# State space decays: one 64-row product a head, one limit by broadcast, four biased exponentials, the gate ahead of them and the scans one step later

## The reference

```
a_cum = cumsum(a, within chunks of 128 tokens)          # a = dt * (-exp(a_log)), 32 heads
seg = a_cum[..., :, None] - a_cum[..., None, :]
decay_in = exp(where(causal, seg, -inf))
cb = einsum('bctgn,bcsgn->bgcts', cc, bc)
y_diag = einsum('bgcts,bgrcts,bcsgrp->bctgrp', cb, decay_in, xc)
decay_to_end = exp(a_cum[..., -1:] - a_cum)
chunk_states = einsum('bctgn,bgrct,bctgrp->bcgrpn', bc, decay_to_end, xc)
# carry the states over the 4 chunks, then
y_off = einsum('bctgn,bcgrpn,bgrct->bctgrp', cc, entering, exp(a_cum))
```

## Time and profile before

| | |
|---|---|
| time, median of 3 runs | 1708.93 us (1708.85 to 1710.78) |
| the profiled execution | 1710.39 us, of which the span of the profile is 1708.6 us |
| TensorE busy | 1669.1 us, 98% of the span |
| VectorE busy | 973.3 us, 57% |
| ScalarE busy | 811.2 us, 47% |
| GpSimd busy | 688.7 us, 40% |
| granted TensorE clock, mean | 0.995 |

### The profile page before, as it was taken

The page is one execution under the profiler, slowest core; times in us unless marked ns, Lnnn a source line. Parts: engine busy times, 40 slices in busy tenths (PEclk is TensorE's granted clock), DMA queues, the critical chain, the costliest instruction groups (busy, mean ns, idle before and its releaser), DMA issues.

```text
span 1708.6 us, 23429 instructions
## 1 busy us (share of the span) xinstructions
PE 1669.1 (98%) x8992; PEld 1349.9 (79%) x8992; DVE 973.3 (57%) x1858; ACT 811.2 (47%) x1370; POOL 688.7 (40%) x905
## 2 busy tenths in 40 slices
PE   8999899999999999998999999999999999999998
PEld 8887567977988888887877777877788777787876
DVE  6489773533665757636656666167453554445445
ACT  5563753532644545424464444145455453534434
POOL 4555323422323342552455556455442333324440
PEclk9999999999999999999999999999999999999999
DMA  8423101221313231411221222211211312112201
GB/s 301 146 102 104 45 2 50 75 74 50 124 49 124 74 135 63 148 62 50 99 75 50 75 75 75 99 62 54 83 64 52 101 51 68 60 52 88 68 27 54
DMA packets 24807, 137.03 MB, mean 80 GB/s; under 512 B 2511, under 2 KB 5839, under 8 KB 11000
## 3 DMA queue, kind: packets, MB, share of 16 engines
q1 hardware_dynamic: 24696, 135.53, 23.0%
HBM read 133.40 MB, written 2.12 MB: 79 GB/s over the span
## 4 chain that ended last, share of the span: by engine, by line
PE 89%; DVE 5%; ACT 3%; issue 1%; DMA 0%; SPq 0%; DVEq 0%; ACTq 0%
PE ps L1660 85%; PE ps L1664 3%; DVE XL L2781 1%; ACT XH L2217 0%; DVE tmp L2708 0%; DVE LNS L2741 0%; PE ps L1668 0%; ACT whi L2217 0%; DVE XL L2785 0%; ACT L2217 0%; DVE ESG L2705 0%; DMA MEM<-memT 0%; DVE LG L2708 0%; DVE mb L2711 0%; ACT tmp L2217 0%
## 5 line engine op out<-in xcount | busy, mean ns | idle before, releaser
L3342 POOL TENSOR_TENSOR wlo<-raw,whi 128x256 fp32r<-128x256 f32 (+1 forms) x820 | 612.9, 784 | 841.2 <-ACT whi L2217 841.2
L2217 ACT ACTIVATE whi<-raw 128x2048 fp32r<-128x2048 f32 (+4 forms) x144 | 248.8, 1731 | 157.7 <-PE ps L1660 122.8
L1660 PE MATMUL ps<-XH,whi 128*128 128x512 f32 (+1 forms) x1176 | 298.5, 374 | 4.4 <-ACT XH L2217 4.2
L1660 PE MATMUL ps<-XL,whi 128*128 128x512 f32 (+1 forms) x1176 | 281.3, 361 | 0.1
L1660 PE MATMUL ps<-XH,wlo 128*128 128x512 f32 (+1 forms) x1176 | 280.6, 361 | 0.0
L1660 PEld LDWEIGHTS ps<-XH,whi 128*128 128x128 f32 x1176 | 200.9, 189 | 43.8 <-ACT XH L2217 6.8
L1660 PEld LDWEIGHTS ps<-XL,whi 128*128 128x128 f32 x1176 | 204.9, 189 | 35.0 <-DVE XL L2785 0.3
L1660 PEld LDWEIGHTS ps<-XH,wlo 128*128 128x128 f32 x1176 | 204.7, 189 | 34.1
L2812 DVE TENSOR_TENSOR R<-ps,R 128x512 f32<-128x512 f32 (+1 forms) x80 | 50.9, 636 | 134.3 <-PE ps L1660 133.7
L1660 PE MATMUL ps<-BH,whi 128*128 128x512 f32 (+1 forms) x320 | 89.4, 397 | 0.0
L1660 PE MATMUL ps<-BL,whi 128*128 128x512 f32 (+1 forms) x320 | 84.1, 380 | 0.8 <-DVE BL L3269 0.8
(11 more groups left out here) (388 smaller groups left out, 2992.5 us busy)
## 6 DMA issues: line engine op xcount, KB each, us to landing
raw<-wall SPq DMA_DIRECT2D x107, 1024.0 KB, 4.8
raw<-wall SPq DMA_DIRECT2D x11, 512.0 KB, 3.5
raw<-wall SPq DMA_DIRECT2D x8, 576.0 KB, 3.6
raw<-wall SPq DMA_DIRECT2D x4, 768.0 KB, 4.2
BFL<-scr SPq DMA_DIRECT2D x2, 1024.0 KB, 8.2
outN<-Y SPq DMA_DIRECT2D x8, 256.0 KB, 2.1
MEM<-memT SPq DMA_DIRECT2D x2, 512.0 KB, 5.0
XTA<-x SPq DMA_DIRECT2D x2, 512.0 KB, 9.4
```

What stands on the lines that cost most here:

```text
L1660: return nc.tensor.matmul(o_, l, r_, start=start, stop=stop, skip_group_check=True)
L2217: return nc.scalar.activation(o_, i_, func, bias=bias, scale=scale)
L3342: t = tt(wlo[u % NSPL][:, c], raw_of(u)[:, c], f32(whi[u % NSPL][:, c]), ALU.subtract)
```

## The change

sx: ACH and ACL become one tile `ACS` of 64 rows, and the identity `IDR` gets 64 rows and the sign -1, so that one product gives minus the spread a_cum. VectorE does one operation a head instead of four: the maximum of that and `NAC` (minus a_cum, broadcast along the chunk). ScalarE's exponentials take the scale -1; that of `ESG` is cut in four, each with its own column of `NAC` as bias. The bank of an sx step is still given back by the first exponential. Order of the list: `gate` is appended ahead of the four sx steps, and `turn` gets one more empty entry in third place, so that each scan piece and g3 and g4 come one main step later. In group 1 the gate and the sx steps of group 0 both stand behind step 4; before, the sx steps stood there and the gate behind step 6.

```diff
@@ -377,10 +377,9 @@
         XDE = [sb(f"XDE{i}", [128, 256]) for i in range(2)]
         BTK = [sb("BTK0", [128, 128], at=rw_at + 128), sb("BTK1", [128, 128])]
         CBM = [sb(f"CBM{i}", [128, 128]) for i in range(2)]
-        IDR = sb("IDR", [32, 32], F32R, at=rw_at)
-        ACH = sb("ACH", [32, T], F32R, at=stat_at)
-        ACL = sb("ACL", [32, T], F32R, at=stat_at + 2048)
-        ACUM = sb("ACUM", [128, 4, 32], at=kt_at + 2048)
+        IDR = sb("IDR", [64, 32], F32R, at=rw_at)
+        ACS = sb("ACS", [64, T], F32R, at=stat_at)
+        NAC = sb("NAC", [128, 4, 32], at=kt_at + 2048)
         DTT = sb("DTT", [32, 6, T], at=top[0])
         ESG = sb("ESG", [128, 4, T])
         ECG = sb("ECG", [128, 4, T - 128])
@@ -855,11 +854,11 @@
             "cv": lambda h: ({"p_cv": 2, "a_cvv": 2, "d_cvv": 2},
                              [x for d in range(2) for x in (("open", ("cv", h, d), "ps"),
                                                             ("close", ("cv", h, d), [("d_cvv", d + 1)]))]),
-            "dc0": lambda: one({"p_dc": 1, "d_dc": 2}, ("dc", 0), "ps", "d_dc"),
-            "dc1": lambda: ({"p_dc": 2, "a_dc": 5, "d_dc": 1},
+            "dc0": lambda: one({"p_dc": 1, "a_dc": 2, "d_dc": 2}, ("dc", 0), "ps", "d_dc"),
+            "dc1": lambda: ({"p_dc": 2, "a_dc": 4, "d_dc": 1},
                             [("open", ("dc", 1), "ps"), ("close", ("dc", 1), [("a_dc", 3)]),
                              ("open", ("dc", 2), "ps"), ("close", ("dc", 2), [("d_dc", 0)])]),
-            "sx": lambda g, h: one({"p_sx": 1, "d_sx": 4, "a_sx": 2}, ("sx", g, h), "ps", "a_sx", 1),
+            "sx": lambda g, h: one({"p_sx": 1, "d_sx": 1, "a_sx": 5}, ("sx", g, h), "ps", "a_sx", 1),
             "gate": lambda g: ({"a_gate": 6}, []),
             "g0": scan0,
             "g1": scan1,
@@ -1397,8 +1396,8 @@
                 emit("sx", g, h)
 
         def group_end(g):
+            emit("gate", g)
             decays(g)
-            emit("gate", g)
 
         def scans(g):
             def chunk(c):
@@ -1434,7 +1433,7 @@
         def turn(g):
 
             tail, scan = gated(g - 1), scans(g)
-            for parts in ((tail,), (), (scan,), (scan,), (tail, scan), (scan,), (scan, tail), (scan,), (scan,), (scan,)):
+            for parts in ((tail,), (), (), (scan,), (scan,), (tail, scan), (scan,), (scan, tail), (scan,), (scan,), (scan,)):
                 for part in parts:
                     next(part)
                 yield
@@ -1449,11 +1448,10 @@
                     next(main)
                 emit("dc1")
                 next(main)
+                emit("gate", 0)
                 decays(0)
-                for _ in range(2):
+                for _ in range(3):
                     next(main)
-                emit("gate", 0)
-                next(main)
                 scan = scans(0)
                 for _ in range(2):
                     next(scan)
@@ -2085,12 +2083,10 @@
 
             def sx(g, h):
                 hd = 4 * g + h
-                one_ = IDR[:, hd:hd + 1].to_broadcast([32, 128])
                 o_ = taken(e, "sx", g, h)
                 e.wait_ge(*on("a_dc", "dc1"))
                 e.wait_ge(*on("d_dc", "dc1"))
-                mm(o_[:, :], one_, ACH[:, :], True, False)
-                mm(o_[:, :], one_, ACL[:, :], False, True).then_inc(S("p_sx"), 1)
+                mm(o_[:, :], IDR[:, hd:hd + 1].to_broadcast([64, 128]), ACS[:, :], True, True).then_inc(S("p_sx"), 1)
 
             def g0(g, c):
                 xs, bt, ct_ = XS[g % 2], BT[g % 2], CTs[g % 2]
@@ -2572,21 +2568,26 @@
                     e.wait_ge(*on("p_cv", "cv", h, i=d + 1))
                     act(BH[:, k, :], slot("cv", h, d)[:, :], ACT.Identity, col("xa_bkv", 8 + k)).then_inc(S("a_cvv"), 1)
 
+            def dc0():
+                for r in (0, 32):
+                    act(IDR[r:r + 32, :], ident[r:r + 32, r:r + 32], ACT.Copy, scale=-1.0).then_inc(S("a_dc"), 1)
+
             def dc1():
                 o_ = slot("dc", 1)
                 e.wait_ge(*on("p_dc", "dc1", i=1))
                 for d, i in ((DTE, 0), (DEC, 1)):
                     act(d[:, :, :], o_[:, 128 * i:128 * i + 128].rearrange("p (c h) -> p c h", c=4), ACT.Exp).then_inc(S("a_dc"), 1)
-                act(ACUM[:, :, :], o_[:, 256:384].rearrange("p (c h) -> p c h", c=4), ACT.Copy).then_inc(S("a_dc"), 1)
+                act(NAC[:, :, :], o_[:, 256:384].rearrange("p (c h) -> p c h", c=4), ACT.Copy, scale=-1.0).then_inc(S("a_dc"), 1)
                 e.wait_ge(*on("p_dc", "dc1"))
                 e.wait_ge(*on("d_xl", "nm", "r0", 1, 2))
-                act(ACH[:, :], slot("dc", 2)[0:32, :], ACT.Copy).then_inc(S("a_dc"), 1)
-                act(IDR[:, :], ident[0:32, 0:32], ACT.Copy).then_inc(S("a_dc"), 1)
+                act(ACS[0:32, :], slot("dc", 2)[0:32, :], ACT.Copy).then_inc(S("a_dc"), 1)
 
             def sx(g, h):
                 e.wait_ge(*on("d_sx", "sx", g, h))
-                act(ECG[:, h, :], slot("sx", g, h)[:, 128:T], ACT.Exp).then_inc(S("a_sx"), 1)
-                act(ESG[:, h, :], ESG[:, h, :], ACT.Exp).then_inc(S("a_sx"), 1)
+                act(ECG[:, h, :], slot("sx", g, h)[:, 128:T], ACT.Exp, scale=-1.0).then_inc(S("a_sx"), 1)
+                for c in range(4):
+                    cc = slice(128 * c, 128 * c + 128)
+                    act(ESG[:, h, cc], ESG[:, h, cc], ACT.Exp, NAC[:, c, 4 * g + h:4 * g + h + 1], -1.0).then_inc(S("a_sx"), 1)
 
             def gate(g):
                 i = g % 2
@@ -2691,7 +2692,7 @@
                     e.wait_ge(*on("p_pj", *last_part(place["mo"][2 * (p // 2 - 1) + 1], 3, None)))
 
             play(dict(init=init, mem=mem, split=split, hb=hb, hs=hs, rb1=rb1, sq=sq, rs=rs, ap=ap, nm=nm, al=al, pj=pj, bt0=bt0, bt1=bt1, ix=ix, va=va,
-                      ex=ex, tu=tu, rc=rc, ss=ss, kl=kl, vl=vl, mv=mv, uv=uv, ce=ce, ct=ct, cv=cv, dc1=dc1, sx=sx,
+                      ex=ex, tu=tu, rc=rc, ss=ss, kl=kl, vl=vl, mv=mv, uv=uv, ce=ce, ct=ct, cv=cv, dc0=dc0, dc1=dc1, sx=sx,
                       gate=gate, g0=g0, g2=g2, g3=g3, g4=g4, lq=lq, lt=lt, kn=kn, vv=vv, zs=zs, qk=qk, pt=pt, pv=pv, fo=fo, fr=fr))
 
 
@@ -3197,7 +3198,7 @@
 
             def dc1():
                 e.wait_ge(*on("a_dc", "dc1", i=4))
-                tt(ACL[:, :], slot("dc", 2)[0:32, :], f32(ACH[:, :]), ALU.subtract).then_inc(S("d_dc"), 1)
+                tt(ACS[32:64, :], slot("dc", 2)[0:32, :], f32(ACS[0:32, :]), ALU.subtract).then_inc(S("d_dc"), 1)
 
             def sx(g, h):
                 hd = 4 * g + h
@@ -3206,9 +3207,8 @@
                 e.wait_ge(*on("a_dc", "dc1"))
                 if g:
                     e.wait_ge(*on("p_y", "g1", g - 1, 3))
-                for c in range(4):
-                    cc = slice(128 * c, 128 * c + 128)
-                    ts(ESG[:, h, cc], o_[:, cc], ACUM[:, c, hd:hd + 1], 0.0, ALU.subtract, ALU.min).then_inc(S("d_sx"), 1)
+                tt(ESG[:, h, :].rearrange("p (c t) -> p c t", c=4), o_[:, :].rearrange("p (c t) -> p c t", c=4),
+                   NAC[:, :, hd:hd + 1].to_broadcast([128, 4, 128]), ALU.max).then_inc(S("d_sx"), 1)
 
             def wide(ap, h, n):
                 return ap.unsqueeze(2).to_broadcast([128, h, n])
```

## The result

| | before | after |
|---|---|---|
| median of 4 runs each, on one chip | 1708.89 us | 1744.17 us (1741.09 to 1745.9) |
| ratio, 95% interval | | 1.0202 (1.019 to 1.0213) |
| span of the profiled run | 1708.6 us | 1743.7 us |
| granted TensorE clock, mean | 0.995 | 0.987 |

The account below looks back on a forecast made before the run. PE, busy 98%, was taken to bound the kernel. Groups 2, 3, 4 and 6 +16.8, group 5 +2.8, group 7 +4.65, group 1 +4.1, behind group 7 +0.7: +29 us, 1738.0 us, range 1720 to 1757.

Parts of the forecast that it names:

- PE's saving: sx on PE: four fewer products a group save about 0.95 us, 7.6 over eight groups.
- The small exponential: sx on ScalarE: each 128-column exponential takes 0.29 us, bounds 0.18 and 0.40; four replace one of 0.53.
- Wait 1: At g1(0) PE waits 1.9 us for DVE's ESG·CBM, with the convolution of tile 1 ahead of g0(0).
- Waits 2 and 3: PE waits for POOL's ECG·CTs behind `wlo`: at g1(1), 1.85 us, and at g1(3), 1.4 us.
- Group 5: +2.8 us (0.8 to 6.4): `so` units lie between, so the wait at g1(3) has cover.
- Group 7's wait 3: At g1(3) of group 7, asked one step nearer, together with g1(2): PE waits 3.7 us.
- Behind group 7: Last scan: g4 of group 6 stands behind its last step and g1(0) moves by +0.7 us (-0.5 to 2.3).
- Group 1's wait: First scan: gate, sx and a convolution stand ahead of g0(0), so PE waits 4.4 us.
- the clock: TensorE's granted clock falls to half speed after the first scan's wait in group 1: 3 us added.
- the clock falls in every group: Rival, chance 0.10: waits of 1.9 us suffice, some 3 us more in six places, 1756 us.
- Gate first: ACT runs gate ahead of sx; sx banks come back 5.84 us later, counted as nothing, 0.8 us left.
- VectorE's one limit: DVE: four 128-column operations a head become one of 512, ready before ScalarE, counted as nothing.

Follow-up runs that it names:

- holding the splits: Changed kernel with each xs and bc split listed behind its step's scan piece instead of ahead (group 5: xs only): 1726.43 us.
- the run with one exponential: Changed kernel with one 512-column exponential a head in place of four of 128, leaving out the column's own sum: 1720.51 us.
- the pause alone: Kernel before with only the extra empty entry in the turn, so scans come one step later: 1732.82 us.
- the arithmetic alone: Kernel before with the one product, one limit and four exponentials, its gate order and scan steps kept: 1733.16 us.
- the place of the pause with the held splits: Changed kernel with splits listed behind their step's scan piece and the empty entry moved to between g0(1) and g1(0): 1714.72 us.
- the run with the later, unheld pause: Changed kernel with the empty entry moved to between g0(1) and g1(0), splits where the change has them: 1732.5 us.
- the change without the pause: Changed kernel with the extra empty entry in the turn taken out again: 1727.69 us.

## Why the prediction was right, and where it was short

*PE's saving*, 0.95 a group: measured 0.94 (eight in 2.05, four in 1.11). But on the kernel before it is worth nothing alone, because of the STT chain; only the pause, or a later g4, makes room for it.

*The small exponential*, 0.29: measured 0.29, with durations of 387 to 413 ns that overlap. The Trainium skill ("VectorE: DVE Perf Modes", "The TRN2 errata", with "ScalarE: Activation LUTs", "What ACT_TABLE_LOAD costs") led to 0.385 if nothing overlapped. The durations, 397 in the middle, agree with that. The second of these sections also says that ScalarE's activations, one behind another, overlap by about 93 ns; an estimate from the two figures is 0.29, and the steps agree with it too. So these pages don't speak against 0.29; the prediction read only half of them. Its own 0.29 had in it 0.03 for the source in SBUF that no row shows; that it came out is in part luck.

*Wait 1*, 1.9: 2.06 to 2.11 in most groups, 1.01 in group 2. That the order on VectorE causes it, the convolution of tile 1 ahead of g0(0), was shown by moving g0(0) back ahead of it. Why group 2 waits only half as long stays open.

*Waits 2 and 3*, 1.85 and 1.4: 1.6 where the clock hadn't fallen, and 1.3 to 2.5. POOL's order was as forecast, and holding the splits took both away. Their causes are shown; their separate prices depend on each other, so that only the sum of a group is a number to rely on: 5.15 forecast, 5.0 in group 3 (2.09, 1.60, 1.31). In groups 4 and 6, where the clock fell behind wait 1, wait 2 vanished and wait 3 grew, and the sum was 4.5 and 4.6. (The slow end of wait 3 was forecast as 3.6; its terms add up to 3.4, which changes nothing here.)

*Group 5*: +2.8 forecast, +2.97. *Group 7's wait 3*: 3.7 forecast, 3.71; on top came a fall of the clock, 3.0 of the 7.83. *Behind group 7*: +0.7 forecast, +1.86, with a wait of 1.09 for BH and one of 1.42 for ECG in the last scan. *Group 1's wait*: 4.4 forecast, 4.37; it is due to the long exponentials ahead of the first scan, as the run with one exponential showed, and its clock fall cost less than my 3: that run had no fall there and a wait of 1.78, so of the 4.15 between the two 1.6 are the clock.

*The term that was mis-sized is the clock.* The sum had one fall, 3 us in group 1. The trace has six: two each in groups 4 and 6 and one each in 1 and 7. What they cost, by the intervals less the waits and the saving: 1.6 each in groups 4 and 6, 3.0 in group 7, where the clock was low for about 7 us and not 3.4, and 1.6 in group 1. That is 11 us against 3, so 8 too little, while the forecast was 6.2 short (1744.2 against 1738.0). The difference is luck: the waits less the saving of groups 2, 3, 4 and 6 came to 14.4 and not 16.8, and the start ahead of the first sx was 1.2 earlier, while the stretch behind group 7 was 1.2 longer. The rival "the clock falls in every group" was half right: it fell in four of seven.

*Gate first* counted as nothing: right in the steady groups, and a gain of 1.2 in group 1. *VectorE's one limit* counted as nothing: the first ECG (992.20) follows the table load (990.90 and 1.28) with no gap, so the limit wasn't waited for; it wasn't tried alone.

The parts don't add. On the kernel before, the pause alone costs 24 and the arithmetic alone 24; with gate first the two together cost 35. Taken the other way, one exponential in place of four gives back 23.7 of the 35.3, and the place of the pause with the held splits gives back 29.5. Both late engines meet the same PE, and either one early enough uncovers less of the other.

Not tried: whether a fitting order for group 1 with the long sx exists. With all of the change's arithmetic the best that ran is 1714.7, 5.9 slower than before, of which group 1 is 3.

## What to carry to other kernels

When a step moves in a program of in-order queues, list for each engine what now stands ahead of it: here one empty entry put 2.2 us of convolution ahead of g0(0) on VectorE and 6 us of weight pieces ahead of two products on GpSimd, and moving it behind g0(1) with the splits held was worth 29.5 us. Before pricing a saving on the busiest engine, look for waits of a tenth or two in its timeline: each is a second chain that will take the saving, and it has to be shortened first. And price waits of one group as one sum, not one by one.

## What the runs showed of the hardware that was not expected

The length of a wait doesn't tell whether TensorE's clock falls behind it. In the run with the later, unheld pause PE waited 2.74 and 2.76 us at g1(3) of two groups and the granted clock stayed at 1.00, and 2.72 and 2.71 in two others and it went to about 0.5. In the run with held splits, 2.06 at 954.65 us had no fall and 2.07 at 1000.86 had one, as its busy time by stretch shows:

```profile
954.00:956.00 2.00, 1.35 (x11) 1.12 (x12) 1.97 (x4) 1.07 (x2) 1.02 (x2) 1.00 0.00 0
956.00:958.00 2.00, 2.00 (x10) 1.68 (x9) 0.43 (x2) 2.00 (x3) 2.00 (x3) 1.00 0.00 0
1002.00:1004.00 2.00, 2.00 (x6) 1.54 (x5) 0.43 (x2) 2.00 (x3) 2.00 (x2) 0.50 0.00 0
```

In group 1 a wait of 1.11 in the kernel before (861.89 us) left it at 1.00, and one of 1.10 with the pause alone (860.68 us) was followed by this stretch:

```profile
862.00:864.00 2.00, 2.00 (x9) 1.90 (x9) 1.39 (x4) 1.98 (x3) 0.61 (x1) 0.50 0.00 0
```

What decides it stays open. A fall costs 1.6 us in most places, as much again as most of the waits; it cost 3.0 in group 7 of the change, and 0.5 in group 6 of the change without the pause, where the interval was 48.35 for 47.8 and the wait of 1.05 for STT behind it was gone. Of the change's 17 waits of 1 us or more from 840 to 1290 us 6 had a fall behind them, and they make some 11 of its 35 us. A forecast that can't tell which waits these are is uncertain by as much.
